# One-hot rows in fp32r: the dense weights of a mixture of single-neuron experts as products of a high and a low part

## The reference

```
top_s, pos = lax.top_k(cand, PEER_TOPK)
idx = jnp.take_along_axis(cidx, pos, axis=-1)        # i1 * 128 + i2
wgt = jax.nn.softmax(top_s, axis=-1)
act = jax.nn.gelu(einsum('bphkd,bpd->bphk', u_tab[ic], xc))
coef = wc * act
out = einsum('bphk,bphkd->bpd', coef, v_tab[ic])
```

## Time and profile before

| | |
|---|---|
| median of three runs | 4454.67 us (4446.75 to 4457.42) |
| profiled execution, span | 4441.0 us |
| TensorE busy | 4275.6 us, 96% |
| VectorE, ScalarE, GpSimd busy | 69%, 41%, 61% |
| hot steps | two stretches, from 1133 to 1637 us and from 3344 to about 3850 us |

### The profile page before, as it was taken

One profiled execution on the slowest core, in us unless ns is written; L12 is line 12 of the kernel. 1 busy time (PEld: TensorE's weight loads), 2 busy tenths in 40 slices (PEclk: granted clock), 3 DMA queues, 4 the chain that ended last, 5 costly groups with the idle time before them and its releaser, 6 DMA issues.

```text
span 4441.0 us, 74459 instructions
## 1 busy us (share of the span) xinstructions
PE 4275.6 (96%) x21290; PEld 3657.1 (82%) x21290; DVE 3081.9 (69%) x5391; ACT 1801.6 (41%) x3318; POOL 2706.0 (61%) x1505
## 2 busy tenths in 40 slices
PE   8999999999999999999999999999999999999998
PEld 6777876779999997777777778767899999978777
DVE  6666435657788767888866664365587887688888
ACT  4145123124576653333341550231246776533333
POOL 6843764765577674555468438647655776645554
PEclk9999999999999999999999999999999999999999
DMA  3233944834699998999822339448346999989997
GB/s 108 90 105 105 270 142 142 231 91 140 200 355 353 315 316 302 339 339 338 288 85 90 110 95 288 134 133 246 87 140 216 348 360 313 308 302 341 344 338 268
DMA packets 494911, 1011.85 MB, mean 228 GB/s; under 512 B 51536, under 2 KB 320464, under 8 KB 491856
## 3 DMA queue, kind: packets, MB, share of 16 engines
q1 hardware_dynamic: 420656, 739.77, 51.9%
q0 software_dynamic: 73728, 268.47, 16.8%
q10 hardware_dynamic: 288, 1.05, 0.1%
HBM read 846.57 MB, written 162.53 MB: 227 GB/s over the span
## 4 chain that ended last, share of the span: by engine, by line
PE 78%; DMA 7%; DVE 5%; issue 3%; ACT 3%; POOL 2%; SPq 1%; DVEq 0%; ACTq 0%; POOLq 0%
PE bank L1366 13%; PE pair L1019 7%; PE bank L1370 6%; PE bank L1019 6%; PE bank L1423 6%; PE bank L1428 6%; DMA ring<-v_tab 5%; PE bank L1418 5%; PE pair L1021 3%; PE bank L1397 3%; PE bank L1045 3%; PE bank L1021 3%; PE pair L1045 2%; PE bank L1086 2%; PE pair L1086 2%
## 5 line engine op out<-in xcount | busy, mean ns | idle before, releaser
L872 POOL TENSOR_TENSOR w_hi<-ring,ones 128x1024 fp32r<-128x1024 f32 x272 | 540.4, 1987 | 696.7 <-PE bank L1045 237.3
L1366 PE MATMUL bank<-xT,w_hi 128*128 128x384 f32 x2048 | 708.1, 346 | 5.1 <-ACT w_hi L1845 3.4
L875 POOL TENSOR_TENSOR w_lo<-ring,w_hi 128x1024 fp32r<-128x1024 f32 x272 | 694.1, 2552 | 21.4
L1366 PE MATMUL bank<-xl_peer,w_hi 128*128 128x384 f32 x2048 | 688.0, 336 | 0.0
L860 POOL TENSOR_TENSOR w_lo<-ring,w_hi 128x1024 fp32r<-128x1024 f32 x192 | 463.0, 2412 | 301.3 <-ACT w_hi L1845 300.4
L1851 ACT CAST w_hi<-ring 128x1024 fp32r<-128x1024 f32 x252 | 265.5, 1054 | 664.8 <-PE bank L1428 450.1
L2724 DVE TENSOR_TENSOR cl<-att,ch 128x384 fp32r<-128x384 f32 x256 | 352.3, 1376 | 165.3 <-ACT ch L1920 152.0
L866 POOL TENSOR_TENSOR w_lo<-ring,w_hi 128x1024 fp32r<-128x1024 f32 x126 | 301.7, 2395 | 266.7 <-ACT w_hi L1851 266.6
L1423 PE MATMUL bank<-w_hi,cl 128*128 128x512 f32 x1524 | 391.3, 392 | 18.6 <-DVE cl L2724 18.6
L1418 PE MATMUL bank<-w_hi,ch 128*128 128x512 f32 x1524 | 389.7, 391 | 12.2 <-ACT ch L1920 11.9
L1370 PE MATMUL bank<-xT,w_lo 128*128 128x384 f32 x2048 | 396.9, 334 | 0.0
(11 more groups left out here) (406 smaller groups left out, 9362.7 us busy)
## 6 DMA issues: line engine op xcount, KB each, us to landing
ring<-v_tab SPq DMA_DIRECT2D x252, 512.0 KB, 6.3
ring<-w_stream SPq DMA_DIRECT2D x240, 512.0 KB, 3.9
g_spill<-gst SPq DMA_DIRECT2D x240, 192.0 KB, 4.5
vg<-w_spill SPq DMA_DIRECT2D x64, 704.0 KB, 10.3
att<-u_tab SPq DMA_DIRECT2D x320, 128.0 KB, 4.6
u_turned<-att SPq DMA_DIRECT2D x80, 512.0 KB, 5.4
ring<-u_tab SPq DMA_DIRECT2D x256, 128.0 KB, 3.0
ring<-u_turned SPq DMA_DIRECT2D x64, 512.0 KB, 5.6
```

Source lines behind the costliest of these rows:

```text
L872: nc.gpsimd.tensor_tensor(w_hi[b][:, 0:n], src, ones[:, 0:1].to_broadcast([P, n]), ALU.mult)\
L875: nc.gpsimd.tensor_tensor(w_lo[b][:, 0:n], src, w_hi[b][:, 0:n].bitcast(F32), ALU.subtract)\
L1366: nc.tensor.matmul(out, w_hi[s % 2][:, c * P:(c + 1) * P], dense_parts(c)[part], start=(c == 0 and part == 0), stop=False)
```

## The change

The weight of a choice is split once at each tile boundary, in the new `split_weights`: `pick_high`, the weight cast to fp32r, and `pick_low`, the remainder divided by `pick_high` (at least 1e-30). Both one-hot matrices become fp32r. VectorE writes `hot2` with one comparison as before, and `hot1` token by token: four instructions that compare and multiply by the token's `pick_high`. ScalarE's four instructions no longer write in place: they read `hot1` and write `hot1_low`, scaled by `pick_low`, in fp32r into a new buffer. TensorE multiplies `hot2` with `hot1` and then with `hot1_low`, adding both in PSUM: eight products in fp32r where there were four in fp32.

```diff
                             for j in range(4):
+                                nc.tensor.matmul(bank[b][:, j * P:(j + 1) * P], hot2[s % 2][:, j, :],
+                                                 hot1[s % 2][:, j, :], start=True, stop=False)
                                 mm = nc.tensor.matmul(bank[b][:, j * P:(j + 1) * P], hot2[s % 2][:, j, :],
-                                                      hot1[s % 2][:, j, :], start=True, stop=True)
+                                                      hot1_low[s % 2][:, j, :], start=False, stop=True)
...
-                        ins = nc.scalar.activation(hot1[b][:, j, :], hot1[b][:, j, :], ACT.Copy,
-                                                   scale=pickw[:, at + j:at + j + 1])
+                        ins = nc.scalar.activation(hot1_low[b][:, j, :], hot1[b][:, j, :].bitcast(F32), ACT.Copy,
+                                                   scale=pick_low[:, at + j:at + j + 1])
...
+                def split_weights(d):
+
+                    c = Chain(dve, pick_step, L, "UW", d)
+                    c.step(V.tensor_copy(pick_first, pickT[:, 0, :]))
+                    c.step(V.tensor_copy(pick_high[:, :], pickT[:, 2, :]))
+                    c.wait()
+                    c.step(V.tensor_tensor(pick_low, pickT[:, 2, :], pick_high[:, :].bitcast(F32), ALU.subtract))
+                    c.step(V.tensor_scalar(pick_inv, pick_high[:, :].bitcast(F32), 1e-30, None, ALU.max))
+                    c.wait()
+                    c.step(V.reciprocal(pick_inv, pick_inv))
+                    c.wait()
+                    c.step(V.tensor_tensor(pick_low, pick_low, pick_inv, ALU.mult))
+                    c.wait()
+                    c.close()
...
                     if k % 8 == 0 and s == 0:
-                        V.tensor_copy(pickw, pickT[:, 2, :])
-                    for z in range(2):
-                        ins = V.tensor_tensor(hot[b][:, z, :, :], pickT[:, z, at:at + 4].unsqueeze(2).to_broadcast([P, 4, N_KEYS]),
-                                              iota_k[:, :].unsqueeze(1).to_broadcast([P, 4, N_KEYS]), ALU.is_equal)
+                        split_weights(k // 8)
+                    V.tensor_tensor(hot2[b], pickT[:, 1, at:at + 4].unsqueeze(2).to_broadcast([P, 4, N_KEYS]),
+                                    iota_k[:, :].unsqueeze(1).to_broadcast([P, 4, N_KEYS]), ALU.is_equal)
+                    for j in range(4):
+                        ins = V.tensor_scalar(hot1[b][:, j, :], iota_k[:, :], pick_first[:, at + j:at + j + 1],
+                                              pick_high[:, at + j:at + j + 1].bitcast(F32), ALU.is_equal, ALU.mult)
                     ins.then_inc(ones_ready.sem, 1)
```

More of the change, by code:

```diff
@@ L247, in build @@
         og = vg[:, KC:2 * KC, :]
+        qk_at = nc.sbuf_base
         qk = sb("qk", [P, 4, SEQ])
+        fox_more_at = nc.sbuf_base
         fox_more = sb("fox_more", [P, 2, SEQ])
@@ L288, in build @@
         gcol = sb("gcol", [P, TT, ML_H])
+        floor_at = nc.sbuf_base
         floor = sb("floor", [P, 2, SEQ])
@@ L291, in build @@
         i_row = floor[0:ML_H, 1, :]
-        pickw = floor[:, 0, 0:P]
+        pick_first = floor[:, 0, 0:P]
+        pick_low = floor[:, 0, P:2 * P]
+        pick_inv = floor[:, 0, 2 * P:3 * P]
+        pick_high = nc.alloc_sbuf_tensor_at("pick_high", [P, P], F32R, offset=floor_at + 4 * SEQ)
         lruw = att[:, 6656:6656 + 8 * P].rearrange("p (s g n) -> p s g n", s=4, g=2)
@@ L366, in build @@
         win = [a[:, 0:4 * (NB - 1) * WB].rearrange("p (b i t) -> p b i t", b=NB - 1, t=WB) for a in win_at]
-        hot = [qk[:, 2 * b:2 * b + 2, :].rearrange("p z (t n) -> p z t n", n=N_KEYS) for b in range(2)]
-        hot1, hot2 = ([hot[b][:, z, :, :] for b in range(2)] for z in range(2))
+        hots = nc.alloc_sbuf_tensor_at("hots", [P, 4, SEQ], F32R, offset=qk_at)
+        hots_low = nc.alloc_sbuf_tensor_at("hots_low", [P, 2, SEQ], F32R, offset=fox_more_at)
+        hot1, hot2 = ([hots[:, 2 * b + z, :].rearrange("p (t n) -> p t n", n=N_KEYS) for b in range(2)] for z in range(2))
+        hot1_low = [hots_low[:, b, :].rearrange("p (t n) -> p t n", n=N_KEYS) for b in range(2)]
         pickT = bank[6][:, 0:3 * P].rearrange("p (a k) -> p a k", a=3)
@@ L486, in build @@
         hot_ready = Count(sem("hot_ready"), dict(UW=(WROUNDS, 4)))
+        pick_step = Count(sem("pick_step"), dict(UW=(DENSE, 6)))
         g_used = Count(sem("g_used"), dict(U=(1, SLOTS), V=(1, SLOTS)))
```

## The result

The changed kernel takes 4721.85 us (median of 4 runs, 4681.15 to 4752.72) against 4454.14 (4446.75 to 4457.42): ratio 1.0575, 95% interval 1.0532 to 1.0618. The forecast was 4509 with a range up to 4565. The sign was right; the loss, 268 us by the medians and 256 by the ratio, is about five times the 54 forecast. One run each of this kernel, of e9 and of e12 fell into a slower state of the chip, and the ratios leave these three out.

A forecast was written before the change was run, and what follows sets the result against it. TensorE, busy for 96% of the span, was taken to set the pace. Boundaries of 8.8 us and locked steps of 18.2 us a layer, over two layers, add 54 us to 4454.7, giving 4509; range 4456 to 4565.

The forecast's parts named there:

- TensorE: nothing.: TensorE's products in a hot step: eight pairs of load and product stay 0.11 us apart, 0.88 us a step, saving 0.
- Rival 4: TensorE's eight one-pass products run at half the distance, up to 0.44 us a step saved, 4433 us; chance 0.10.
- Rows of 1.49 us, 0.20 apart.: VectorE in a hot step: comparison plus four row instructions take 1.49 us, 0.2 more, fitting into 0.7 to spare.
- While VectorE is a step ahead, it merely slides.: VectorE's rows waiting for GpSimd's w_lo start later until they miss it; 4.2 us plus 0.2 fit into 5.08.
- The boundaries, 8.8 us a layer: Tile boundaries: VectorE's one copy becomes a chain of 2.4 us; three boundaries add 8.8 us a layer, 17.6 in all.
- d = 0: Tile boundary where TensorE already waits 3.89 us for ScalarE's rows: 2.4 us added, the pause becoming 6.3.
- d = 1: Tile boundary where the chain's last product waits for w_lo, so TensorE's products start 3.2 us later.
- d = 2: Tile boundary with the same shape as d = 1: 3.2 us later.
- The ring: Hot steps after d = 1: engines lock, rows wait for w_lo, steps of 5.8 us, 26 of 64, 18.2 a layer.
- Rival 3: VectorE's four instructions cost 0.5 us more a step with waits besides, ring step 6.1, 4550 to 4600 us; chance 0.12.
- Rival 1: Hot steps: the ring does not hold, VectorE regains its lead, only the boundaries cost, 4473 us; chance 0.17.
- Rival 2: GpSimd and VectorE's four instructions do not disturb each other, 9.6 us in all, 4464 us; chance 0.13.

The follow-up runs named there:

- e9: Changed kernel with the comparison ahead of the four row instructions on 112 of every 128 columns, so the rows start 0.07 us earlier: 4655.87 us, ratio 1.0445.
- e12: Kernel before with eight one-pass fp32r products in place of four fp32 ones, without VectorE's rows or the boundary chain: 4455.56 us, ratio 1.0007.
- e5: Kernel before with fp32r one-hots and four one-pass products per step, the low part of the weight left out: 4429.20 us, ratio 0.9931.
- e4: Kernel before with only the four row instructions from SBUF to SBUF, one pointer and immediate 1.0, fp32 products, no chain: 4481.75 us, ratio 1.0051.
- e6: Changed kernel with the immediate 1.0 in place of the row instructions' second pointer, the one to the high part: 4505.62 us, ratio 1.0119.
- e1: Changed kernel with the four row instructions reading the key numbers from PSUM, copied there once a tile: 4514.54 us, ratio 1.0133.
- e3: Kernel before with only the chain of six weight-splitting instructions at a tile's start, its low part unused: 4479.86 us, ratio 1.0058.
- e7: Kernel before with only the four row instructions, fp32 products, no chain, and a second pointer, to the weight: 4718.24 us, ratio 1.0588.
- e10: Kernel before with only the four row instructions, one pointer, delayed some 0.2 us by one unused copy from PSUM: 4678.83 us, ratio 1.0505.
- e2: Changed kernel with GpSimd's w_lo in hot steps written for 128 of its 1024 columns: 4481.90 us, ratio 1.0051.
- e8: Changed kernel with the four row instructions ahead of VectorE's comparison in place of behind it: 4534.23 us, ratio 1.0175.

## Why the prediction was wrong, step by step

- **TensorE: nothing.** Right. A pair of load and product takes as long in either type (e12), and e5 confirms its price, 0.11 us. Rival 4 (half the distance) falls; its cap by the DMA share of 0.95 would not have held either, since e5's steps with gathers stand at 4.63 us. The Trainium skill's 81 ns for such a pair (TensorE: Matmul & The Clock Gate, "Back-to-back issue gap"), weighed in the prediction, is not what these rows show: they show 0.11 us.
- **Rows of 1.49 us, 0.20 apart.** Mis-sized: 0.26 apart and 0.34 long, 1.72 us, just under the upper bound of 1.76. The row it was taken from has one pointer operand and does stand for one (e4, e6: 0.20); the second costs 0.06 each. The prediction treated this as an amount of work, 0.2 us with 0.7 to spare. As an amount it is cheap: e1's rows take 1.97, and e1 is only some 35 us above e3. As a position it decided most of the result.
- **"While VectorE is a step ahead, it merely slides."** Right where TensorE sets the rhythm (steps 40 to 63 of the first layer, 5.06 us with groups of rows held up to 2.9 us), and why e4 and e6 cost so little.
- **The boundaries, 8.8 us a layer.** The mechanism was right, and so were its sizes. d = 0: TensorE's pause was forecast at 6.3 us and is 6.4. d = 1: forecast 3.2, of which 0.2 for the rows; e3 shows 8.49 - 5.41 = 3.1, with the product waiting for `w_lo`, and the same at d = 2. As a sum e3 loses 26 to 28 us against 17.6 for both layers; the rest lies outside the boundary steps and is in part too small to tell from the difference between two executions of one kernel.
- **The ring: the step that failed.** "The engines can lock in a ring" was right; its step, its extent and its condition were not. I had the four coming at 3.6 us, in the middle of `w_lo`, waiting 1.3 and giving a step of 5.8, in 26 of 64 steps because I took a lead lost at a boundary for its cause. A lead lost to the chain is neither needed nor enough: e7 and e10 have no chain and lock; in the changed kernel the fourth is held in the steps 15 to 28, midway in a tile; and e6 has the chain and does not lock behind a boundary. What ties the ring is that one event of VectorE's releases both partners: the transposing releases the comparison and rows, and, through the cast, `w_lo`. They then meet at a fixed distance, at the fourth instruction and the very start of `w_lo`, so each time the fourth lasts 2.45 us instead of 0.34 (3.0 with a gather ahead), and it delays the next transposing or dot product, that is, the event itself. Steps are 6.4 us in the last stretch and 8.0 in steps 14 to 31, not 5.8. Extra in the 95 steps from first to last: 607.7 - 495.5 = 112 us in the first layer and 635.2 - 497.2 = 138 in the second, against a forecast of 27 a layer with the boundaries.
- **Rivals.** Rival 3 (dearer instructions, ring step 6.1, 4550 to 4600) was nearest and still over 110 us low, since it too had the rows come in the middle of `w_lo`. Rival 1 (only the boundaries, 4473) is what e3 and e2 show: 4480 and 4482. Rival 2 (no disturbance) falls with the 146 held groups.
- **A small term.** The 13.7 us between the profiled span and the median were read as what lies around the span. In each of the thirteen kernels that followed the time of the profiled run is only 1.7 to 1.8 us above its span; the other 12 are the difference between one execution and the median. The forecast of 4509 is not touched, as the 54 us were added to the median.

The shares, by the ratios: chain 0.6% (e3), rows at 0.20 us 0.6% (e6 less e3; e4 alone 0.5%), the second pointer 4.6% (changed kernel less e6; e7 less e4 5.4%), TensorE nothing (e12).

**What stays open.** How near a gather must be for the fourth instruction to be held. At 1299.35 in the changed kernel it starts 0.47 us into a gather and waits; in another step the fourth starts at 1422.64, 0.35 into one, and runs freely:

```profile
1421.88 1.11 DVE L2687 TENSOR_SCALAR hots<-iota_k,floor,pick_high 128x128 fp32r<-128x128 f32 x4
```

In e10 both occur at one distance from `w_lo`, 0.58 us ahead. In the changed kernel all 57 row instructions that start inside a gather and last over 1 us start 0.35 to 0.54 us into it, but 45 others that start in that interval last less. So the edge at `w_lo`'s start was shown, that at the gather only bracketed. What starts a run of locked steps was not shown either: the fourth is held from step 15 on in the changed kernel, from step 22 in e7. Nor was it tried why steps 40 to 63 lock in one layer and not in the other (129.8 and 174.4 us in the changed kernel), or what TensorE's lower clock adds to the locked stretches; VectorE's 92 to 100% there says that it is not what bounds them.

## What to carry to other kernels

Where VectorE and GpSimd instructions can hold each other up, ask not only how much work an edit adds but which event releases each partner: if one event releases both, they meet at the same point in every step, and a few hundredths of a microsecond can decide between nothing and the partner's whole duration. Look for it in the trace by the place in a group at which the long instruction stands, and try the cheap cures first: the same instructions in another order (e8 took back 188 of 268 us by the medians), one operand fewer, or an input from PSUM. And an fp32 product of 128 columns made into two one-pass fp32r products, each with its own load, costs TensorE the same (e12).

## What the runs showed of the hardware

- A VectorE instruction of 128 x 128 from SBUF with one pointer operand takes 0.28 us and starts 0.20 behind the one before; with two pointers 0.34 and 0.26; with input from PSUM and two pointers 0.40 and 0.32, and none of 768 waits for GpSimd (e1). fp32r as output changes nothing (e6).
- GpSimd can start between two such instructions that stand back to back, and the next then waits for the whole of it (1585.83 and 2.39 us above). The edge lies where the VectorE instruction starts 0.040 to 0.048 us ahead (e9). The other way round GpSimd's instruction took 0.13 us longer, and nothing longer at 0.16 us ahead (e4, 2.39 us).
- Eight one-pass fp32r products of 128 columns with their loads take as long as four fp32 ones: 0.11 us for each pair (e12, e5).
